# Two of six weight units per expert loaded ahead into spare memory and copied into the ring, with the refills of the spare memory issued behind the ring's loads from the fourth expert on

## The chip, the core and the metric

The kernel runs on one core of a Trainium2 chip. The metric is the device time of one launch in microseconds (us), the median of several runs. TensorE (PE) does the matrix products, VectorE (DVE), ScalarE (ACT) and GpSimd (POOL) the elementwise work. Each engine runs its own list of instructions in order and waits on semaphores for the others. SyncE (SP) issues most of the transfers from device memory (HBM) into the on-chip memory.

## What is computed

Two layers of a backbone over 128 context and 512 latent tokens of width 1024, all in float32. Each layer is an attention and convolution part, and then a mixture of 16 experts that choose their own tokens. The change is in the mixture:

```python
def expert_choice(h, w_router, w_gate, w_up, w_down):
    B, T, D = h.shape
    C = EC_FACTOR * T // N_EXPERTS
    aff = jax.nn.softmax(jnp.einsum('btd,de->bte', h, w_router).astype(jnp.float32), axis=-1)
    gsel, idx = lax.top_k(aff.transpose(0, 2, 1), C)
    xs = jax.vmap(lambda hb, ib: hb[ib])(h, idx)
    hid = jax.nn.silu(jnp.einsum('becd,edf->becf', xs, w_gate)) * jnp.einsum('becd,edf->becf', xs, w_up)
    ye = jnp.einsum('becf,efd->becd', hid, w_down) * gsel[..., None].astype(h.dtype)
    return jax.vmap(lambda yb, ib: jnp.zeros((T, D), yb.dtype).at[ib.reshape(-1)].add(yb.reshape(-1, D)))(ye, idx)
```

Each expert picks C = 64 latent and 16 context tokens, 80 columns together. It has three matrices of 1024 x 1024 float32, six times 2 MB. All 16 experts of both layers are read once, 192 units of 2 MB.

## The kernel before, in words

**Units and the ring.** An expert's weights come in six units of 2 MB: 0 is the first half of w_gate, 1 the first half of w_up, 2 and 3 the second halves, 4 and 5 the halves of w_down. I write e.i for unit i of expert e. The ring (`weight_ring`) has six slots of 2 MB, and unit i always goes to the slot `UNIT_SLOTS[l][i]` of layer l. So e.i can be loaded when TensorE is done with (e-1).i, which it tells through the semaphore `expert_used`.

**SP** first issues the six units of expert 0, while the attention part still runs. It stores and reloads the chosen token numbers (`picks`, `pick_row`) and the gains. Then a hardware loop over experts 1 to 15 waits for `expert_used` and issues one unit after the other (`expert_unit`, L404), always in the order 0 to 5.

**TensorE** runs, for each expert, `gate_up(e)` (units 0 to 3, 128 matmuls each, L868), waits for `picked_lo_ready` and `picked_hi_ready` ahead of it, and then `down(e)` (units 4 and 5, L885), whose first half waits for the hidden values (`hid_ready`).

**ScalarE**, for each expert, in order: wait until unit 2 is used, two SiLU operations over the gate's products (L1145, L1147); wait until unit 3 is used, then gather 48 of the next expert's 80 token columns (`pick_hi(e + 1)`, L1139).

**VectorE** multiplies SiLU by the up products (`gated_hidden`, L1554), scales the result (`gated_result`, L1569), and adds 48 of the 80 result columns onto the tokens (`add_hi`, L1578). **GpSimd** gathers the other 32 columns (`pick_lo`, L1699) and adds 32 of the result columns (`add_lo`, L1710). For every 8 columns an engine first loads 8 token numbers into registers (L322).

**After the last expert** of layer 0 the tokens are transposed back and layer 1 begins. After that of layer 1, the final norm (L558, L1158, L1596, L1605) is computed with the gain row in `x_norm`, which was loaded at the start of the expert stage, and the result is stored.

Of the kernel before, what the change touches and what calls it, by code (L numbers as in the profile page):

```python
# [17 lines left out]
EXPERTS, D_EXP = 16, 1024  # L18
# [42 lines left out]
PICK_SPLIT = 32  # L61
PICK_LOAD = 8

# [14 lines left out]
def build(nc, x_prompt, x_sample, c, cache_k, cache_v, c_ctx, norm1_g, w_mod, b_mod, w_in, conv_w, conv_b,  # L78
# [9 lines left out]
    with ctx:  # L88
# [32 lines left out]
        result_t = u_gate[:, 2 * D:2 * D + KD * CAP].rearrange("p (k n) -> p k n", k=KD)  # L121
# [7 lines left out]
        x_tile_flat = x_tile[:, :, :].rearrange("p b n -> p (b n)")  # L129
        pick_row = x_tile_flat[0:1, 0:EXPERTS * CAP].bitcast(u32)  # L130
        result_gain = x_tile_flat[:, EXPERTS * CAP:EXPERTS * CAP + KD * CAP].rearrange("p (k n) -> p k n", k=KD)
# [12 lines left out]
        cos_sb = sb("cos_sb", [P, N_LAT])  # L144
        sin_sb = sb("sin_sb", [P, N_LAT])
# [12 lines left out]
        o_tok_flat = o_tok[:, :, :, :].rearrange("p b h n -> p (b h n)")  # L158
        lam_rows = o_tok_flat[:, 0:DEPTH * 4 * HD].rearrange("p (l f n) -> p l f n", l=DEPTH, f=4)
# [50 lines left out]
        expert_used = signal("expert_used", 6 * EXPERTS)  # L210
        mod_rows_done = signal("mod_rows_done", len(MOD_LIST[0]))
# [71 lines left out]
        picks_loaded = signal("picks_loaded", 1, 16)  # L283
# [35 lines left out]
        def picks_of(engine, e, at, n):  # L319

            src = top_i[0:1, at:at + n] if e == 0 else pick_row[:, e * CAP + at:e * CAP + at + n]
            return nc.values_load_multi_w_load_instructions(  # L322
                src, engines=[engine], min_val=0, max_val=(N_LAT if at < CAP_LAT else N_CTX) - 1,
                skip_runtime_bounds_check_because="max_index counts within the row that it searched")[1]

# [54 lines left out]
        def _(sp):  # L380
# [21 lines left out]

            def expert_unit(l, e, i):
# [5 lines left out]
            for l in range(DEPTH):  # L409
# [50 lines left out]

                sp.wait_ge(*top_round.at(l, TOP_ROUNDS))
# [3 lines left out]
                sp.dma_start(pick_row, picks.rearrange("(a e) n -> a (e n)", a=1)).then_inc(picks_loaded.sem, 16)  # L465
# [18 lines left out]
        def _(pe):  # L484
# [20 lines left out]
            def past_transposes():  # L505

                pe.wait_ge(*misc_loaded.at(0, 4 * DEPTH + 3 * DEPTH + 2))
# [395 lines left out]
        def _(act):  # L903
# [27 lines left out]
            for l in range(DEPTH):  # L931
# [199 lines left out]
                def pick_hi(e):  # L1131

                    for at in range(PICK_SPLIT, CAP, PICK_LOAD):
                        if e == 0:
                            act.wait_ge(*top_round.at(l, at // 8 + 1))
                        elif e == 1 and at == PICK_SPLIT:
                            act.wait_ge(*picks_loaded.at(l, 1))
# [27 lines left out]
        def _(dve):  # L1165
# [27 lines left out]
            def setup_lambda():  # L1193

                dve.wait_ge(*misc_loaded.at(0, 4 * DEPTH + 3 * DEPTH + 2))
# [20 lines left out]
            for l in range(DEPTH):  # L1216
# [120 lines left out]
                def rotate(i):  # L1337
                    x = (k_t, q_t)[i][:, :, N_CTX:N_TOK]
                    for h in range(H):
# [3 lines left out]
                    nc.vector.tensor_tensor(x, x, cos_sb[:].unsqueeze(1).to_broadcast([P, H, N_LAT]), ALU.mult)  # L1343
                    own(step(nc.vector.tensor_tensor(rope_tmp, rope_tmp,
                                                     sin_sb[:].unsqueeze(1).to_broadcast([P, H, N_LAT]), ALU.mult)))
# [235 lines left out]
                dve.wait_ge(*picks_loaded.at(l, 1))  # L1581
# [29 lines left out]
        def _(pool):  # L1611
# [25 lines left out]
            def load_misc():  # L1637
# [10 lines left out]
                pool.dma_start(cos_sb[:], rope_cos).then_inc(misc_loaded.sem, 16)  # L1648
# [120 lines left out]
```

## Time and profile before

| | us |
|---|---|
| median of 3 runs | 1874.3 |
| the three runs | 1874.30, 1870.84, 1879.41 |
| the profiled execution | 1873.58 |
| its span in the trace | 1871.8 |
| expert stage of layer 0, first matmul to last | 442.8 to 931.4 |
| expert stage of layer 1, first matmul to last | 1356.3 to 1844.9 |

The two expert stages take 977 of the 1872 us. In the profile's 40 slices of 46.8 us each they are slices 10 to 19 and 30 to 39. There the moved bytes per second stand at one level, and TensorE's busy share is 8 or 9 tenths. The views to read are the slices, the chain of work that ended last, the timeline of SP and of TensorE, and the wait times; the rows are two sections below.

### The profile page before, as it was taken

Reading aid. Unit: us, or ns where it says so; the run is one execution under the profiler, and the core shown is the slowest. Engines: PE = TensorE matmul, PEld = TensorE weight load, DVE = VectorE, ACT = ScalarE, POOL = GpSimd, SP = SyncE. Lnnn points to the kernel's source line nnn. Section 1 sums busy time; section 2 is a strip of 40 time slices with the busy share of each in tenths; the row PEclk is TensorE's granted clock in tenths of the full one; section 3 lists DMA queues with packets and bytes.
Section 4 is the critical chain, followed back from the end, with each engine's and each line's share of the span. In section 5 each row is a group of like instructions: output and inputs, shape, how many; then the busy total and the mean of one; then the engine's idle time right before and its main releaser. Section 6 shows DMA issues by size and latency. Waiting matters only on the chain. (4 is left out here: it accounts for less than half of the span.)

```text
span 1871.8 us, 69942 instructions
## 1 busy us (share of the span) xinstructions
PE 1651.7 (88%) x27933; PEld 1303.6 (70%) x27933; DVE 815.4 (44%) x2591; ACT 446.5 (24%) x2106; POOL 373.3 (20%) x2131
## 2 busy tenths in 40 slices
PE   6999988996999888888859999889599998888885
PEld 3555456455999888888745444665389988888885
DVE  2299477244323323222245983853623232323233
ACT  2200155322221212121130012552312212121211
POOL 1100000001333423232210000000123333333331
PEclk9999989997999999999979999999799999999998
DMA  9447540224999999999921551320389999999992
GB/s 349 126 167 240 209 169 1 101 83 179 400 409 409 409 409 409 409 409 407 369 106 45 180 184 62 149 87 26 118 324 410 409 409 409 409 409 409 409 407 105
DMA packets 145011, 502.04 MB, mean 268 GB/s; under 512 B 4643, under 2 KB 5060, under 8 KB 144870
## 3 DMA queue, kind: packets, MB, share of 16 engines
q1 hardware_dynamic: 140740, 488.95, 67.3%
q0 software_dynamic: 3104, 10.36, 1.7%
q10 hardware_dynamic: 1026, 1.25, 0.2%
q8 instruction: 39, 0.64, 0.1%
q14 instruction: 102, 0.84, 0.1%
HBM read 494.23 MB, written 6.31 MB: 267 GB/s over the span
## 5 line engine op out<-in xcount | busy, mean ns | idle before, releaser
L868 PE MATMUL ps<-v_sb,weight_ring 128*64 128x80 f32 x16384 | 592.4, 234 | 70.7 <-DMA weight_ring<-in_w_gate_dram 26.6
L868 PEld LDWEIGHTS ps<-v_sb,weight_ring 128*64 128x64 f32 x16384 | 576.6, 138 | 86.2 <-DMA weight_ring<-in_w_gate_dram 33.2
L885 PE MATMUL ps<-v_sb,weight_ring 128*64 128x80 f32 x8192 | 296.4, 233 | 33.9 <-DVE v_sb L1554 19.6
L885 PEld LDWEIGHTS ps<-v_sb,weight_ring 128*64 128x64 f32 x8192 | 287.2, 137 | 43.1 <-DVE v_sb L1554 25.4
L640 PE MATMUL ps<-mix,weight_ring 128*128 128x128 f32 (+1 forms) x976 | 270.0, 437 | 4.4 <-DVE mix L1258 3.2
L1578 DVE TENSOR_TENSOR qk<-qk,u_gate 128x8 f32 x1536 | 209.2, 188 | 97.6 <-issue 95.9
L1139 ACT ACTIVATE v_sb<-mix 128x8 f32 x1536 | 187.1, 205 | 231.9 <-PE ps L868 150.9
L1699 POOL COPY v_sb<-mix 128x8 f32 x1024 | 143.0, 198 | 490.1 <-PE ps L868 432.9
L640 PEld LDWEIGHTS ps<-mix,weight_ring 128*128 128x128 f32 x976 | 147.5, 193 | 126.3 <-issue 121.0
L1710 POOL TENSOR_TENSOR qk<-qk,u_gate 128x8 f32 x1024 | 184.3, 219 | 212.3 <-DVE u_gate L1569 199.2
L1330 DVE SCALAR_TENSOR_TENSOR weight_ring<-u_gate,conv_cols,weight_ring 128x655 f32<-128x655 f32 x240 | 195.3, 894 | 0.0
L1554 DVE TENSOR_TENSOR v_sb<-v_sb,ps 128x320 f32<-128x320 f32 x64 | 28.3, 484 | 314.8 <-PE ps L868 314.8
L1569 DVE TENSOR_TENSOR u_gate<-ps,x_tile 128x320 f32<-128x320 f32 x64 | 31.5, 492 | 286.2 <-PE ps L885 286.2
L779 PE MATMUL ps<-weight_ring,mix 128*128 128x512 f32 x320 | 143.1, 603 | 0.0
L1145 ACT ACTIVATE v_sb<-ps 128x320 f32<-128x320 f32 x32 | 14.0, 438 | 522.0 <-PE ps L868 522.0
L779 PEld LDWEIGHTS ps<-weight_ring,mix 128*128 128x128 f32 x320 | 60.7, 194 | 71.1 <-issue 71.1
L677 PE MATMUL ps<-weight_ring,mix 128*128 128x512 f32 x160 | 70.5, 595 | 0.0
L1401 DVE TENSOR_REDUCE neg_m<-ps 128x2 f32<-128x1280 f32 (+1 forms) x40 | 50.8, 1274 | 16.1 <-PE ps L714 15.5
L1060 ACT ACTIVATE weight_ring<-ps,neg_m 128x640 f32<-128x640 f32 (+1 forms) x80 | 55.8, 707 | 3.2 <-DVE neg_m L1401 3.2
L677 PEld LDWEIGHTS ps<-weight_ring,mix 128*128 128x128 f32 x160 | 29.7, 190 | 36.5 <-issue 36.5
L1635 POOL DMA_DIRECT2D x_tile<-x_res x5 | 2.9, 574 | 250.9 <-PE ps L537 170.7
L725 PE MATMUL ps<-ident,weight_ring 128*128 128x128 f32 x168 | 33.4, 305 | 18.7 <-DVE o_tok L1420 9.0
(179 smaller groups left out, 1150.3 us busy)
## 6 DMA issues: line engine op xcount, KB each, us to landing
weight_ring<-in_w_gate_dram SPq DMA_DIRECT2D x64, 2048.0 KB, 23.8
weight_ring<-in_w_up_dram SPq DMA_DIRECT2D x64, 2048.0 KB, 23.8
weight_ring<-in_w_down_dram SPq DMA_DIRECT2D x64, 2048.0 KB, 24.5
weight_ring<-in_w_mod_dram SPq DMA_DIRECT2D x24, 2048.0 KB, 8.5
weight_ring<-in_w_in_dram SPq DMA_DIRECT2D x10, 2048.0 KB, 10.8
weight_ring<-in_w_out_dram SPq DMA_DIRECT2D x4, 2048.0 KB, 9.4
x_tile<-x_res POOLq DMA_DIRECT2D x5, 512.0 KB, 3.6
out_dram<-mix SPq DMA_DIRECT2D x5, 512.0 KB, 3.2
```

What stands on the lines that cost most here:

```text
L640: last = nc.tensor.matmul(ps[:, 2 * (n % 3) + bank, 0:cols.stop - cols.start], w[:, k, tokens(b)], mix[:, k, cols], start=(k == 0), stop=( ...
L677: last = nc.tensor.matmul(ps[:, 2 * (n % 3), :], mix[:, k, tokens(t)], w[:, k, :], start=(k == 0), stop=(k == KD - 1))
L779: last = nc.tensor.matmul(ps[:, 2 * (i % 2) + n, :], mix[:, k, tokens(t)], w[:, k % 4, n * BANK:(n + 1) * BANK], start=(at == 0), stop=(at ...
L868: last = nc.tensor.matmul(ps[c * HALF:(c + 1) * HALF, 2 * (i % 2) + f // BLK, f % BLK * CAP:(f % BLK + 1) * CAP], w[:, kk, o:o + HALF], pi ...
L885: last = nc.tensor.matmul(ps[c * HALF:(c + 1) * HALF, 4 + d // BLK, d % BLK * CAP:(d % BLK + 1) * CAP], w[:, kk, o:o + HALF], hid[:, k, :] ...
L1060: last = nc.scalar.activation(prob[:, b, m, 0:n], score_rows(s)[:, m, :], ACT.Exp, bias=neg_m[:, b, m:m + 1], accum_out=row_sum[:, b, m:m ...
L1139: last = nc.scalar.activation(picked_t[:, :, j:j + 1], picked_row(j, pick), ACT.Copy)
L1330: ins = nc.vector.scalar_tensor_tensor(acc[:, j, :], src, w, acc[:, j, :], ALU.mult, ALU.add)
L1401: nc.vector.tensor_reduce(neg_m[:, s % 2, :], score_rows(s), AX, ALU.max, negate=True)\
L1578: last = nc.vector.tensor_tensor(x, x, result_t[:, :, j:j + 1], ALU.add)
L1699: last = nc.gpsimd.tensor_copy(picked_t[:, :, j:j + 1], picked_row(j, pick))
L1710: last = nc.gpsimd.tensor_tensor(x, x, result_t[:, :, j:j + 1], ALU.add)
```

## The change

Three things are joined.

**Relayed units.** Units 0 and 1 of experts 1 to 15 are no longer loaded straight into the ring. SP loads each as four pieces of 512 KB (one DMA each) into eight buffers of 128 x 1024 (`relay`), made of a new tensor `spare`, the rotary tables' memory, `o_tok`, and parts of `u_gate`, `x_tile`, `conv_tmp` and `x_norm` that are idle in this stage. When TensorE has used unit r of expert e-1, ScalarE copies the four pieces into the ring slot (`relay_copy(e, r)`) and then raises `expert_loaded[r]`. The relays of expert 1 are issued before the experts begin. The relays of expert e+1 (`refill_relays(e + 1)`) are issued ahead of units 2 to 5 of expert e for e below 4, and behind them from e = 4 on (`RELAY_FIRST`). Since the rotary tables are overwritten, GpSimd reloads them in layer 1, and the gain row of the final norm is loaded after the last expert.

**Evened last adds.** For the last expert the 80 result columns are split 40 and 40 instead of 32 (GpSimd) and 48 (VectorE) (`LAST_SPLIT`).

**Early index registers.** `add_hi` and `add_lo` load the first 8 token numbers ahead of the wait for the result. The token numbers lie in four partitions, loaded by four small DMAs instead of one, and the result tile moves from `u_gate` to `v_sb`.

```diff
+LAST_SPLIT = 40
+RELAYS = 2
+RELAY_FIRST = 4
+RELAY = KD // 2
...
+        relay = ((spare[:, 0, :], spare[:, 1, :], rope_sb[:, :, :].rearrange("p b n -> p (b n)"), o_tok_flat),
+                 (u_gate[:, EXPERTS * CAP:EXPERTS * CAP + D], x_tile[:, 1, :], conv_tmp_flat[:, 0:D], x_norm[:]))
...
+            def relay_piece(l, e, r, j):
+                sp.dma_start(relay[r][j], expert_src(l, e, r)[:, j, :]).then_inc(relay_loaded[r].sem, 16)
...
+                for r in range(RELAYS):
+                    if r == 1:
+                        sp.wait_ge(*x2_ready.at(l, TILES))
+                        sp.wait_ge(*ssq2_ready.at(l, TILES))
+                        sp.wait_ge(*x2_transposed.at(l, TILES - 1))
+                    for j in range(RELAY):
+                        relay_piece(l, 1, r, j)
...
-                with sp.Fori(1, EXPERTS) as e:
-                    for i in range(6):
-
+                def refill_relays(e):
+
+                    for r in range(RELAYS if e < EXPERTS else 0):
+                        for j in range(RELAY):
+                            if j < RELAY - 1:
+                                sp.wait_ge(*relay_copied[r].at(l, (e - 2) * (RELAY - 1) + j + 1))
+                            else:
+                                sp.wait_ge(*expert_loaded[r].at(l, e))
+                            relay_piece(l, e, r, j)
+
+                for e in range(1, EXPERTS):
+                    if e < RELAY_FIRST:
+                        refill_relays(e + 1)
+                    for i in range(RELAYS, 6):
                         sp.wait_ge(*expert_used.at(l, e * 6 + (i - 5)))
                         expert_unit(l, e, i)
+                    if e >= RELAY_FIRST:
+                        refill_relays(e + 1)
...
+                def relay_copy(e, r):
+                    act.wait_ge(*expert_used.at(l, (e - 1) * 6 + r + 1))
+                    act.wait_ge(*relay_loaded[r].at(l, e * RELAY))
+                    w = ring[:, UNIT_SLOTS[l][r], :].rearrange("p (j n) -> p j n", j=RELAY)
+                    for j in range(RELAY - 1):
+                        nc.scalar.activation(w[:, j, :], relay[r][j], ACT.Copy).then_inc(relay_copied[r].sem, 1)
+                    nc.scalar.activation(w[:, RELAY - 1, :], relay[r][RELAY - 1], ACT.Copy)\
+                      .then_inc(expert_loaded[r].sem, 16)
+
                 pick_hi(0)
                 for e in range(EXPERTS):
+                    if e + 1 < EXPERTS:
+                        for r in range(RELAYS):
+                            relay_copy(e + 1, r)
                     act.wait_ge(*expert_used.at(l, e * 6 + 3))
...
                 def add_hi(e):
-                    dve.wait_ge(*result_taken.at(l, e + 2))
-                    for at in range(PICK_SPLIT, CAP, PICK_LOAD):
-                        for j, pick in enumerate(picks_of(mybir.EngineType.DVE, e, at, PICK_LOAD), at):
+                    for at in range(add_split(e), CAP, PICK_LOAD):
+                        rows = picks_of(mybir.EngineType.DVE, e, at, PICK_LOAD)
+                        if at == add_split(e):
+                            dve.wait_ge(*result_taken.at(l, e + 2))
+                        for j, pick in enumerate(rows, at):
...
+            pool.wait_ge(*expert_loaded[1].at(DEPTH - 1, EXPERTS))
+            pool.dma_start(x_norm[:], final_norm_g.rearrange("(a n) -> a n", a=1).to_broadcast([P, D]))\
+                .then_inc(gain_loaded.sem, 16)
```

**Where the instructions stand, ScalarE.** First ScalarE between the last gather for one expert and the first gather for the next, before the change. `v_sb<-mix` is one gathered column, `v_sb<-ps` a SiLU, `x_tile` the load of token numbers into registers.

```order
L1139 ACTIVATE v_sb<-mix 128x8
L1145 ACTIVATE v_sb<-ps 128x320 [waits expert_used]
L1147 ACTIVATE v_sb<-ps 128x320
L322 TENSOR_LOAD x_tile [waits expert_used]
L1139 ISA
```

And after the change, at the same place:

```order
L1178 ACTIVATE v_sb<-mix 128x8
L1186 ACTIVATE weight_ring<-spare 128x1024 [waits relay_loaded0,expert_used]
L1186 ACTIVATE weight_ring<-spare 128x1024
L1186 ACTIVATE weight_ring<-rope_sb 128x1024
L1187 ACTIVATE weight_ring<-o_tok 128x1024
L1186 ACTIVATE weight_ring<-u_gate 128x1024 [waits relay_loaded1,expert_used]
L1186 ACTIVATE weight_ring<-x_tile 128x1024
L1186 ACTIVATE weight_ring<-conv_tmp 128x1024
L1187 ACTIVATE weight_ring<-x_norm 128x1024
L1196 ACTIVATE v_sb<-ps 128x320 [waits expert_used]
L1198 ACTIVATE v_sb<-ps 128x320
L332 TENSOR_LOAD x_tile [waits expert_used]
```

Eight copies of 128 x 1024 and two waits for landed relays now stand ahead of the two SiLU operations; the copies are of the next expert's units, the SiLU is the present expert's.

**SP.** The second place is SP's expert loop. Before, one pass of the hardware loop:

```order
L404 ISA [waits expert_used]
L404 DMA weight_ring<-in_w_gate_dram 128x4x1024
L473 REGISTER_ALU
L404 DMA weight_ring<-in_w_up_dram 128x4x1024 [waits expert_used]
L473 REGISTER_ALU
L404 ISA [waits expert_used]
L404 DMA weight_ring<-in_w_gate_dram 128x4x1024
L473 REGISTER_ALU
L404 DMA weight_ring<-in_w_up_dram 128x4x1024 [waits expert_used]
L473 REGISTER_ALU
L404 DMA weight_ring<-in_w_down_dram 128x4x1024 [waits expert_used] x2
```

After the change, one pass for an expert e from 4 on (units 2 to 5 of e, then the pieces of units 0 and 1 of e+1):

```order
L420 DMA weight_ring<-in_w_gate_dram 128x4x1024 [waits expert_used]
L420 DMA weight_ring<-in_w_up_dram 128x4x1024 [waits expert_used]
L420 DMA weight_ring<-in_w_down_dram 128x4x1024 [waits expert_used] x2
L417 DMA spare<-in_w_gate_dram 128x1024 [waits relay_copied0] x2
L417 DMA rope_sb<-in_w_gate_dram 128x1024 [waits relay_copied0]
L417 DMA o_tok<-in_w_gate_dram 128x1024 [waits expert_loaded0]
L417 DMA u_gate<-in_w_up_dram 128x1024 [waits relay_copied1]
L417 DMA x_tile<-in_w_up_dram 128x1024 [waits relay_copied1]
L417 DMA conv_tmp<-in_w_up_dram 128x1024 [waits relay_copied1]
L417 DMA x_norm<-in_w_up_dram 128x1024 [waits expert_loaded1]
```

Units 0 and 1 of the next expert have moved from the head of the next pass to the end of this one, as eight transfers, and they wait for ScalarE's copies instead of for TensorE.

## Rows read from the trace of the kernel before

**Rows 1.** The page: busy time by engine, then the 40 slices.
```profile
PE 1651.7 (88%) x27933; PEld 1303.6 (70%) x27933; DVE 815.4 (44%) x2591; ACT 446.5 (24%) x2106; POOL 373.3 (20%) x2131
PE   6999988996999888888859999889599998888885
DMA  9447540224999999999921551320389999999992
```

**Rows 2.** Windows of layer 1's expert stage: us, busy by engine, PEclk, DMA share, GB/s.
```profile
1400.00:1500.00 100.00, 97.66 (x2792) 96.71 (x2788) 29.99 (x171) 26.52 (x200) 35.18 (x224) 1.00 1.03 409
1500.00:1840.00 340.00, 302.42 (x8340) 292.12 (x8334) 100.42 (x582) 66.97 (x502) 108.04 (x672) 1.00 1.00 397
```

**Rows 3.** Chain of work that ended last, layer 1: start us, us, what.
```profile
1418.04 17.87 PE ps L868 x512
1435.94 0.50 DVE v_sb L1554
1436.48 9.07 PE ps L885 x256
...
1815.14 24.97 DMA weight_ring<-in_w_down_dram
1840.23 4.67 PE ps L885 x128
1844.92 0.50 DVE u_gate L1569
```

**Rows 4.** Timeline of SP, the first issue of layer 1's loop.
```profile
1363.44 0.41 SPq L404 DMA_DIRECT2D weight_ring<-in_w_gate_dram  x1
```

**Rows 5.** Line L404 at 1318.7, alone in the queue; then at 1363.4.
```profile
L404 SPq DMA_DIRECT2D weight_ring<-in_w_down_dram x1: 367/367/367, 1318.7 to 1318.7; - x1
...
DMA to landing us min/median/max: 7.6/7.6/7.6
...
L404 SPq DMA_DIRECT2D weight_ring<-in_w_gate_dram x1: 405/405/405, 1363.4 to 1363.4; - x1
...
DMA to landing us min/median/max: 8.9/8.9/8.9
```

**Rows 6.** ScalarE's groups by form: busy us, mean ns of one, idle before.
```profile
L1145 ACT ACTIVATE v_sb<-ps 128x320 f32<-128x320 f32 x32 | 14.0, 438 | 522.0 <-PE ps L868 522.0
L1094 ACT ACTIVATE x_norm<-x_tile 128x1024 f32<-128x1024 f32 x10 | 10.5, 1046 | 27.8 <-DVE x_tile L1462 27.8
```

**Rows 7.** Windows around idle TensorE: after layer 0's last expert, at layer 1's first.
```profile
931.40:934.40 3.00, 0.00 (x0) 0.00 (x0) 1.69 (x10) 0.00 (x0) 1.67 (x10) 1.00 1.05 396
934.40:937.50 3.10, 0.00 (x0) 0.00 (x0) 2.29 (x16) 0.00 (x0) 2.81 (x17) 0.51 1.03 376
...
1356.30:1361.00 4.70, 4.70 (x70) 4.70 (x72) 0.83 (x1) 1.07 (x1) 0.00 (x0) 0.50 0.40 143
1361.00:1363.40 2.40, 2.40 (x72) 2.40 (x70) 0.00 (x0) 0.00 (x0) 0.00 (x0) 0.98 0.00 0
```

**Rows 8.** Timeline after the last expert of layer 1, GpSimd, VectorE, TensorE.
```profile
1846.18 1.54 POOL L1710 TENSOR_TENSOR qk<-qk,u_gate 128x8 f32 x8 [25.28 <-DVE u_gate L1569]
1846.19 1.08 DVE L1578 TENSOR_TENSOR qk<-qk,u_gate 128x8 f32 x8 [0.78 <-DVE u_gate L1569]
1848.01 4.48 POOL L1710 TENSOR_TENSOR qk<-qk,u_gate 128x8 f32 x24 [0.28 <-issue]
1853.20 1.00 DVE L1578 TENSOR_TENSOR qk<-qk,u_gate 128x8 f32 x8 [0.58 <-issue]
1854.78 1.00 DVE L1578 TENSOR_TENSOR qk<-qk,u_gate 128x8 f32 x8 [0.58 <-issue]
1855.92 4.53 PE L558 MATMUL ps<-ident,qk 128*128 128x128 f32 x24 [11.05 <-DVE qk L1578]
1859.12 0.15 DVE L1596 TENSOR_SCALAR mean_sq<-ssq 128x1 f32<-128x1 f32 x1 [3.34 <-ACT conv_tmp L1158]
```

**Rows 9.** DMA issues by line: KB each, us from issue to landing.
```profile
x_norm<-in_final_norm_g_dram POOLq DMA_DIRECT2D x1, 512.0 KB, 3.6
```

More of the change, by code:

```diff
@@ L143, in build @@
         o_sq = conv_tmp[:, 1, 0:BANK].rearrange("p (h n) -> p h n", h=H)
-        cos_sb = sb("cos_sb", [P, N_LAT])
-        sin_sb = sb("sin_sb", [P, N_LAT])
+        rope_sb = sb("rope_sb", [P, 2, N_LAT])
+        cos_sb, sin_sb = rope_sb[:, 0, :], rope_sb[:, 1, :]
+        spare = sb("spare", [P, 2, D])
         past_k_t = sb("past_k_t", [P, DEPTH, H, PAST])
@@ L210, in build @@
         expert_used = signal("expert_used", 6 * EXPERTS)
+        relay_loaded = [signal(f"relay_loaded{r}", RELAY * (EXPERTS - 1), 16) for r in range(RELAYS)]
+        relay_copied = [signal(f"relay_copied{r}", (RELAY - 1) * (EXPERTS - 1)) for r in range(RELAYS)]
+        rope_loaded = signal("rope_loaded", unit=16)
         mod_rows_done = signal("mod_rows_done", len(MOD_LIST[0]))
@@ L282, in build @@
         picks_stored = signal("picks_stored", 1, 16)
[L283 removed]
+        picks_loaded = signal("picks_loaded", 4, 16)
         gains_stored = signal("gains_stored", 1, 16)
@@ L319, in picks_of @@
         def picks_of(engine, e, at, n):
-            src = top_i[0:1, at:at + n] if e == 0 else pick_row[:, e * CAP + at:e * CAP + at + n]
+            row, col = STRIP * (e // 4), (e % 4) * CAP + at
+            src = top_i[0:1, at:at + n] if e == 0 else pick_rows[row:row + 1, col:col + n]
             return nc.values_load_multi_w_load_instructions(
@@ L324, in picks_of, with add_split @@
                 skip_runtime_bounds_check_because="max_index counts within the row that it searched")[1]
+        def add_split(e):
+            return PICK_SPLIT if e + 1 < EXPERTS else LAST_SPLIT
         def picked_row(j, pick):
@@ L464, in _ @@
                 sp.wait_ge(*picks_stored.at(l, 1))
-                sp.dma_start(pick_row, picks.rearrange("(a e) n -> a (e n)", a=1)).then_inc(picks_loaded.sem, 16)
+                for q in range(4):
+                    sp.dma_start(pick_rows[STRIP * q:STRIP * q + 1, :],
+                                 picks[4 * q:4 * q + 4, :].rearrange("(a e) n -> a (e n)", a=1))\
+                      .then_inc(picks_loaded.sem, 16)
                 sp.wait_ge(*gains_stored.at(l, 1))
@@ L1337, in rotate @@
                 def rotate(i):
+                    dve.wait_ge(*rope_loaded.at(0, 2 * (l + 1)))
                     x = (k_t, q_t)[i][:, :, N_CTX:N_TOK]
@@ L1579, in add_hi @@
                     last.then_inc(added_hi.sem, 1)
-                dve.wait_ge(*picks_loaded.at(l, 1))
+                dve.wait_ge(*picks_loaded.at(l, 4))
                 dve.wait_ge(*gains_loaded.at(l, 1))
@@ L1664, in _ @@
                     load_misc()
+                else:
+                    pool.wait_ge(*expert_loaded[0].at(l - 1, EXPERTS))
+                pool.dma_start(cos_sb, rope_cos).then_inc(rope_loaded.sem, 16)
+                pool.dma_start(sin_sb, rope_sin).then_inc(rope_loaded.sem, 16)
                 pool.wait_ge(*mod_cols_done.at(l, mod_groups(l)))
@@ L1702, in add_lo @@
                 def add_lo(e):
-                    pool.wait_ge(*result_taken.at(l, e + 2))
-                    if e > 0:
-                        pool.wait_ge(*added_lo.at(l, e))
-                        pool.wait_ge(*added_hi.at(l, e))
-                    for at in range(0, PICK_SPLIT, PICK_LOAD):
-                        for j, pick in enumerate(picks_of(mybir.EngineType.Pool, e, at, PICK_LOAD), at):
+                    for at in range(0, add_split(e), PICK_LOAD):
+                        rows = picks_of(mybir.EngineType.Pool, e, at, PICK_LOAD)
+                        if at == 0:
+                            pool.wait_ge(*result_taken.at(l, e + 2))
+                            if e > 0:
+                                pool.wait_ge(*added_lo.at(l, e))
+                                pool.wait_ge(*added_hi.at(l, e))
+                        for j, pick in enumerate(rows, at):
                             x = residual_row(j, pick)
```

24 lines of the change are left out of this document (9 added, 15 removed).

## The prediction

> **What bounds the kernel now.** I read the slices first. In both expert stages DMA stands at 9 tenths in every slice, and PE at 8 or 9 [rows 1]. The windows tell the two phases apart: up to 1500 TensorE is busy 97.66 of 100 us, later 302.42 of 340, while the transfers never pause [rows 2]. So TensorE lives at first on the six units that were loaded ahead, uses them up, and from 1500 on waits for each unit to land. The chain confirms it: one expert takes TensorE 17.87 + 0.50 + 9.07, with seams 27.5 us [rows 3], and the last link of the chain is a unit's landing, 4.67 us of matmuls, and VectorE [rows 3].
>
> The transfer side: the first unit of the loop is issued at 1363.44 [rows 4] and lands 8.9 us later, at 1372.3 [rows 5]. The last is issued at 1815.14 and lands at 1840.11 [rows 3]. Those are units 1 and 90 of layer 1's loop, so a unit takes 467.8 / 89 = 5.26 us, and six take 31.5 us, against TensorE's 27.5. **The stage ends when its 90 units are through, and only two things can shorten it: fewer units after the start, or an earlier start.**
>
> **The part that ought to gain.** Two units of expert 1 now land before the stage, in time when DMA is mostly idle (slices 28 and 29, digits 0 and 3 [rows 1]). 88 units are left: 2 x 5.26 = 10.5 us per layer. The stream can start only when ScalarE has copied the first relayed piece, one 128 x 1024 operation of 1.05 us [rows 6]; 9.5 us per layer would be left if the stream then stayed full.
>
> **Does it stay full? Experts 1 to 3: yes.** SP issues 2.0, 2.1, 1.2 to 1.5, 3.0, 3.1, 2.2 to 2.5, 4.0, 4.1, 3.2 to 3.5, then 4.2 to 4.5, 5.0, 5.1. With the first landing at 1373.3 and 5.26 us each, 3.2 lands at 1373.3 + 14 x 5.26 = 1446.9. Expert 2 begins at 1418.04 [rows 3] and expert 3 27.5 us later, at 1445.5, and wants 3.2 another 9 us later. So TensorE runs at its own 27.5 us and ScalarE finds the relays landed. Its work per expert grows by 8 copies, about 8 us, in a queue that is 24% busy [rows 1]; two copy groups of 3.9 us fit into the 4.5 us that each unit of matmuls takes. I price that at nothing. What hides it is TensorE's own unit time.
>
> **From expert 4 on: no.** ScalarE's list is in order, and the copies of the next expert's units 0 and 1 stand ahead of the present expert's SiLU. Both copies wait for landed relays, and from expert 4 on SP issues those relays behind all of the present expert's units. So down(e) cannot start before (e+1).1 has landed, three units after e.4, which TensorE wants next. Let X(e) be the landing of (e+1).1.
>
> - X(4) is the 24th landing: 1373.3 + 23 x 5.26 = 1494.2. Before, TensorE was at down(4) at 1418.04 + 2 x 27.5 + 17.9 = 1490.9.
> - After X: four copies. A 128 x 1024 operation takes 1.05 us [rows 6], and overlapped ones some 0.95 (an estimate: the operation less the part that the next one hides): 3.9 us. SiLU 0.44 [rows 6], VectorE's product 0.50 [rows 3], two hand-overs of 0.05. TensorE starts unit e.4 at X + 4.95.
> - e.4 takes 4.65 us. Its slot is then free, and SP, which has stood there, issues (e+1).4 after 0.15. By then the stream, which needed this issue when (e+1).3 began to drain, has only (e+1).3's tail left: X + 9.75 against the end of (e+1).3 at X + 10.5 (and with the clock term below, nothing).
> - Landing a unit from an empty queue took 7.6 and 8.9 us [rows 5]; I take the middle, 8.3, since the queue is nearly, not wholly, empty. Then (e+1).5, (e+2).0 and (e+2).1 follow at 5.26.
>
> **The loop closes:** X(e+1) = X(e) + 4.95 + 4.65 + 0.15 + 8.3 + 15.8 = X(e) + 33.85 us. That is 2.3 more than the stream's own 31.5, for every expert from 4 to 14.
>
> **TensorE's clock.** Per expert TensorE works 27 us and then stands for 6 to 7 us ahead of down(e). After layer 0's last expert it stood from 931.4, and the granted clock was 1.00 up to 934.4 and 0.51 after, that is 1.2 instead of 2.4 GHz [rows 7]. When layer 1's experts began it was at 0.50 for the first 4.70 us and 0.98 after [rows 7], and the first unit took until 1363.3 [rows 4], 7.0 instead of 4.65 us. I take it that the clock falls in each of these pauses and that e.4 pays 2.1 us, a little less than the 2.4 seen. The period is then 35.95 us. The Trainium skill's page "TensorE: Matmul & The Clock Gate", section "HAM oscillation — how this bites in real kernels", describes such a loop, in which every tile's wait for data puts the array back to half rate; the expert stage before the change shows granted clock 1.00 throughout [rows 2], so only the new pause can bring it.
>
> **The end of a stage.** X(14) = 1494.2 + 10 x 35.95 = 1853.7. Then 4.95 to down(14), 9.3 + 2.1 for it, and all of expert 15, whose weights now come early enough, at 27.5: 1897.6. Before it was 1844.9 [rows 3]. **+52.7 us in layer 1**, and the same in layer 0, whose stage had the same length (488.6 us both).
>
> A second page of the Trainium skill, "DMA: Bandwidth & Descriptors", bears on this in its section "Rules for kernel authors": issue early, compute, and wait on the semaphore late. ScalarE here waits early, ahead of work that others need. The section "Anatomy of one DMA" of that page of the Trainium skill puts the fixed cost of a transfer at about 2.0 us; by that the landing would be 5.26 + 2.0 = 7.3, the period 34.95, and each stage 10 us shorter than forecast, an estimate. The rows here show 7.6 and 8.9, and I stay with them.
>
> **Last adds and index registers.** VectorE added 48 columns from 1846.19 to 1855.8, 1.58 us for each 8 ([rows 8], 1853.20 to 1854.78), and GpSimd was through with its 32 at 1852.5. With 40 and 40, VectorE saves one group, 1.6 us, and the register load ahead of the first, 0.6 of the 0.78 idle [rows 8]; GpSimd needs 6.3 / 4 = 1.6 more and starts 0.6 earlier, so it ends at about 1853.5. The end moves by 2.2 us in each layer. In layer 1 the gain row is now issued by GpSimd when it is done, and took 3.6 us to land [rows 9]; VectorE wants it 3.3 us after the last add ([rows 8], 1855.8 to 1859.12). So 0.5 us is given back there. Sum: -2.2 - 1.7 = -3.9. Elsewhere the early registers lie beside waiting.
>
> **Edits at no cost.** Four picks DMAs instead of one: SP is 1 us later with the gains, which VectorE needs only for down(0), 20 us later. Reloading the rotary tables: 512 KB at the start of layer 1, where DMA shows digits 2, 1 and 5 [rows 1], long ahead of their use.
>
> **Sum:** profiled execution 1873.6 + 2 x 52.7 - 3.9 = 1975.1. Its time is within 1 us of the median 1874.3, so I forecast the same for a median.
>
> **Rivals.**
> 1. *The clock holds at 2.4 GHz* through the pauses. Then the period is 33.85 and the stage ends at 1494.2 + 338.5 + 4.95 + 9.3 + 27.5 = 1874.5, +29.6 per layer: 1873.6 + 59.2 - 3.9 = 1929. For it: the pause is 6 to 7 us, and the pause in the rows was 11. Against: it had fallen 3 us into that one [rows 7].
> 2. *The loop hides in the stream*: a free slot is reported just early enough and each issue overlaps what is in flight. The period is 31.5; TensorE is still three units behind the stream at the end: 1494.2 + 315.4 + 4.95 + 9.3 + 27.5 = 1851.4, +6.5 per layer, 1883. The issue would have to come 3 us before the stream needs it; it comes 0.8 us before.
> 3. *Faster*: ScalarE is not in the way, because the stream at expert 4 is already three units further ahead than I reckon, and stays there. Then 2 x 9.5 + 3.9 us are gained: 1851. It decides at X(4): 5.1 would have to land before 1490.9 - 4.95 = 1486, 8 us earlier than reckoned. In the rows TensorE gains 4 us per expert on the stream, so such a lead melts within three experts. That speaks against it.
> 4. *The relays do not run ahead at all*, for want of a free buffer. The order of waits gives no reason.
>
> **How the numbers follow.** Forecast 0.66, rival 1 0.22, rival 2 0.05, rival 3 0.06, rest 0.01. For the range: low side with no clock loss, 7.6 for the landing and 5.13 per unit (2.1 MB at the 409 GB/s of [rows 2]): period 32.7, +18 per layer, 1906. High side with 8.9 for the landing, 2.4 for the clock and copies that don't overlap (4.2): period 37.15, +65 per layer, 1873.6 + 130 - 3.9 = 2000. So 1908 to 2000. Faster by over 0.5% (what a measurement of this kernel can tell) 0.07, within 0.5% 0.03, slower 0.90.
>
> **What would show it.** In the timeline of an expert from 5 on: ScalarE idle until a relay has landed, copies, and only then SiLU; TensorE idle 6 to 7 us ahead of each down, none between units; a period of 36 us; the granted clock below 1 in these pauses; DMA share under 1 in slices that were full; SP's waits for `expert_used` long, and its issues short. Experts 1 to 3 at 27.5 us. I would be wrong if TensorE waited for units and not for hidden values, or if DMA stayed at its level to the end.

## The result and the profile after

| | before, us | after, us |
|---|---|---|
| median of 4 runs | 1873.16 | 1985.28 |
| lowest to highest | 1870.84 to 1879.41 | 1979.50 to 1991.72 |
| the profiled execution, and its span | 1873.58, 1871.8 | 1987.45, 1985.5 |

The ratio is 1.0599, with a 95% interval from 1.0572 to 1.0625: **slower by 6%**. Forecast were 1975 us, with 1908 to 2000 as the range. The spans differ by 113.7 us.

The page of the changed kernel, as in [rows 1]: busy time by engine, then the slices, here of 49.6 us, with PEclk, the granted clock in tenths.

```profile
PE 1682.6 (85%) x27933; PEld 1349.1 (68%) x27933; DVE 819.4 (41%) x2575; ACT 668.8 (34%) x2346; POOL 390.8 (20%) x2149
PE   6999988958988788788859999899599778778786
PEclk9999988979988989889979999999799879988888
DMA  9346342059999989989831552121699989989982
```

TensorE does the same 27933 matmuls, but takes 31 us longer for them (1682.6 against 1651.7). PE has 7s where it had 8s and 9s. ScalarE has 240 instructions more, the copies: 15 experts x 8 x 2 layers. DMA shows 8s among the 9s.

Layer 1's expert stage in windows, as in [rows 2]. Columns: us, busy PE, PEld, DVE, ACT, POOL, granted clock, DMA share, GB/s. The first is experts 3 and 4 up to the first pause, the second runs from there to just behind the last relay's landing (1916.28).

```profile
1504.00:1551.00 47.00, 44.06 (x1264) 43.66 (x1260) 16.55 (x102) 17.78 (x62) 18.00 (x105) 1.00 1.01 395
1551.00:1917.00 366.00, 291.96 (x7680) 289.30 (x7680) 93.41 (x530) 139.87 (x582) 107.12 (x643) 0.88 0.89 346
```

Before, the stream ran at a share of 1.00 and 397 GB/s to the end. Now it does so only until TensorE stops for the first time; from there on 346 GB/s and a clock of 0.88.

The chain of work that ended last, as in [rows 3]: start us, us, what.

```profile
1448.33 17.76 PE ps L907 x512
1466.65 9.07 PE ps L924 x256
1475.73 17.87 PE ps L907 x512
...
1536.47 16.24 DMA x_norm<-in_w_up_dram
1557.65 11.11 PE ps L924 x256
1573.30 15.62 DMA x_norm<-in_w_up_dram
1593.87 11.74 PE ps L924 x256
1610.54 15.59 DMA x_norm<-in_w_up_dram
```

The rows from 1448.33 on are experts 1 and 2: experts 1 to 3 follow each other at 27.5 us (1448.33 to 1475.73 is 27.4), with matmuls alone. From expert 4 on the chain alternates: the last piece of the relayed unit 1 (`x_norm`), ScalarE, `down` (L924), again such a piece. These landings, the X(4) to X(14) of the prediction, are at 1552.71, 1588.93, 1626.13 and so on to 1916.28: ten periods in 363.57 us, 36.36 us each.

One period on TensorE and ScalarE, in their timelines: start us, us, what, and in brackets the idle time ahead and its releaser.

```profile
1557.65 11.08 PE L924 MATMUL ps<-v_sb,weight_ring 128*64 128x80 f32 x256 [9.01 <-DVE v_sb L1606]
1568.65 17.93 PE L907 MATMUL ps<-v_sb,weight_ring 128*64 128x80 f32 x512
1593.87 11.71 PE L924 MATMUL ps<-v_sb,weight_ring 128*64 128x80 f32 x256 [7.29 <-DVE v_sb L1606]
```
```profile
1583.90 2.00 ACT L1186 ACTIVATE weight_ring<-spare 128x1024 f32<-128x1024 f32 x2 [19.97 <-DMA o_tok<-in_w_gate_dram]
...
1589.01 1.06 ACT L1186 ACTIVATE weight_ring<-u_gate 128x1024 f32<-128x1024 f32 x1 [1.21 <-DMA x_norm<-in_w_up_dram]
...
1591.87 1.04 ACT L1187 ACTIVATE weight_ring<-x_norm 128x1024 f32<-128x1024 f32 x1
1592.81 0.41 ACT L1196 ACTIVATE v_sb<-ps 128x320 f32<-128x320 f32 x1
```

TensorE is done with the gate and up products at 1586.6 (1568.65 + 17.93). Their SiLU (L1196) runs at 1592.81, because ScalarE stands at the copy of the next expert's unit 1 until 1589.01 and then makes four copies. The wait is not one for weights: TensorE goes through the 512 matmuls of units 0 to 3 without a gap, and units 4 and 5 of this expert have landed too (1572.15 and 1578.71, from the rows below).

SP's issues in the same period, then the two units of w_down on their way to landing.

```profile
1564.35 4.79 SPq L420 DMA_DIRECT2D weight_ring<-in_w_down_dram  x2
1573.30 1.20 SPq L417 DMA_DIRECT2D x_norm<-in_w_up_dram  x1
```
```profile
DMA to landing us min/median/max: 7.8/7.8/7.8
```
```profile
DMA to landing us min/median/max: 9.9/9.9/9.9
```

The first was issued at 1564.35, when TensorE had used unit 4 of the expert before, the second at 1568.77. Ahead of them the stream ran dry (columns as above):

```profile
1560.00:1562.00 2.00, 2.00 (x38) 2.00 (x36) 0.00 (x0) 1.35 (x12) 0.00 (x0) 0.54 0.39 156
1562.00:1564.00 2.00, 2.00 (x65) 2.00 (x61) 0.00 (x0) 1.52 (x14) 0.00 (x0) 1.00 0.02 6
1564.00:1566.00 2.00, 2.00 (x64) 2.00 (x60) 0.00 (x0) 0.00 (x0) 0.00 (x0) 1.00 0.24 33
```

By the three shares some 4.7 us of a full stream are missing here (an estimate), about what a period is longer than the stream's 31.5. SP had transfers that were free to go: ScalarE's copies had emptied all eight relay buffers by 1556.7 (1555.65 + 1.04), but their refills stand behind these two units in SP's list.

The clock, in a window on the end of this pause (1553 to 1558), in one on the next pause and in one on the `down` behind that (columns as above):

```profile
1553.00:1558.00 5.00, 0.35 (x6) 0.35 (x8) 0.89 (x2) 5.00 (x14) 1.75 (x13) 0.50 1.03 410
1589.00:1592.50 3.50, 0.00 (x0) 0.00 (x0) 0.00 (x0) 3.49 (x4) 2.62 (x20) 0.52 1.02 406
1592.50:1599.40 6.90, 5.53 (x84) 5.53 (x86) 0.88 (x2) 5.79 (x45) 0.63 (x5) 0.50 0.82 327
```

In each of the eleven pauses of layer 1, 6.3 to 9.0 us long, the granted clock falls to 0.50, the lower of its levels (1.2 GHz), and it stays there for the first 2.7 to 6.0 us of the work behind: `down` takes 10.3 to 11.9 us, 11.4 in the mean, instead of 9.07.

The waits summed over both layers: who waited for what, us, times, longest.

```profile
PE ps L924 <- DVE v_sb L1606: 168.6, 32, 9.0
...
ACT weight_ring L1186 <- DMA o_tok<-in_w_gate_dram: 441.1, 22, 21.2
```

**Where the 113.7 us are.** Layer 0's expert stage takes 549.4 us instead of 488.6 (+60.8), layer 1's 545.8 (+57.2). Between the stages it is 1.9 less, behind the last 2.1 less, ahead of the first 0.3 less: 118.0 - 4.3 = 113.7.

### The profile page after: what moved, and what is told of

Its sections match the earlier page's. It is cut to its first block and busy times, and to the rows that moved or that the text cites. A ratio compares the mean times of both kernels' runs of the same rounds, so it can differ in the third digit from the quotient of the medians.

```text
span 1985.5 us, 69965 instructions
## 1 busy us (share of the span) xinstructions
PE 1682.6 (85%) x27933; PEld 1349.1 (68%) x27933; DVE 819.4 (41%) x2575; ACT 668.8 (34%) x2346; POOL 390.8 (20%) x2149
## 5 line engine op out<-in xcount | busy, mean ns | idle before, releaser
L907 PE MATMUL ps<-v_sb,weight_ring 128*64 128x80 f32 x16384 | 579.0, 234 | 17.9 <-ACT v_sb L1178 15.6
L907 PEld LDWEIGHTS ps<-v_sb,weight_ring 128*64 128x64 f32 x16384 | 573.7, 138 | 21.9 <-issue 19.3
L924 PE MATMUL ps<-v_sb,weight_ring 128*64 128x80 f32 x8192 | 341.9, 254 | 173.5 <-DVE v_sb L1606 168.6
L924 PEld LDWEIGHTS ps<-v_sb,weight_ring 128*64 128x64 f32 x8192 | 336.0, 155 | 179.4 <-DVE v_sb L1606 173.8
L1768 POOL TENSOR_TENSOR qk<-qk,v_sb 128x8 f32 x1040 | 200.2, 234 | 361.4 <-DVE v_sb L1621 358.8
L1632 DVE TENSOR_TENSOR qk<-qk,v_sb 128x8 f32 x1520 | 212.1, 194 | 90.5 <-issue 89.7
L1186 ACT ACTIVATE weight_ring<-spare 128x1024 f32<-128x1024 f32 x60 | 60.1, 1049 | 493.7 <-DMA o_tok<-in_w_gate_dram 441.1
L1178 ACT ACTIVATE v_sb<-mix 128x8 f32 x1536 | 180.4, 205 | 87.1 <-issue 43.9
L1621 DVE TENSOR_TENSOR v_sb<-ps,x_tile 128x320 f32<-128x320 f32 x64 | 31.5, 492 | 321.7 <-PE ps L924 321.7
L1035 ACT ACTIVATE qk<-ps 128x512 f32<-128x512 f32 x16 | 9.6, 598 | 153.1 <-PE ps L679 153.1
## 6 DMA issues: line engine op xcount, KB each, us to landing
weight_ring<-in_w_gate_dram SPq DMA_DIRECT2D x34, 2048.0 KB, 11.9
```

Source lines behind the costliest of these rows:

```text
L907: last = nc.tensor.matmul(ps[c * HALF:(c + 1) * HALF, 2 * (i % 2) + f // BLK, f % BLK * CAP:(f % BLK + 1) * CAP], w[:, kk, o:o + HALF], pi ...
L924: last = nc.tensor.matmul(ps[c * HALF:(c + 1) * HALF, 4 + d // BLK, d % BLK * CAP:(d % BLK + 1) * CAP], w[:, kk, o:o + HALF], hid[:, k, :] ...
L1178: last = nc.scalar.activation(picked_t[:, :, j:j + 1], picked_row(j, pick), ACT.Copy)
L1186: nc.scalar.activation(w[:, j, :], relay[r][j], ACT.Copy).then_inc(relay_copied[r].sem, 1)
L1632: last = nc.vector.tensor_tensor(x, x, result_t[:, :, j:j + 1], ALU.add)
L1768: last = nc.gpsimd.tensor_tensor(x, x, result_t[:, :, j:j + 1], ALU.add)
```

## The experiments

Two readings were held against each other. **The loop:** ScalarE waits for the next expert's relays ahead of the present SiLU, SP issues those relays behind units that TensorE frees only after this SiLU, and so landing, copy, SiLU, `down` and issue make one closed chain that is longer than the stream needs. **The rivals:** the relays as such (eight small transfers, copies through ScalarE, traffic in the memories) cost the time; or the clock alone does. Ratios are against the kernel before, run on the same chip beside each.

### e1: the relays always first

```diff
-RELAY_FIRST = 4
+RELAY_FIRST = 16
```

> The changed kernel with one number changed: the relays of the next expert are issued ahead of the present expert's units 2 to 5 for all experts (RELAY_FIRST 16), as the changed kernel does for experts 1 to 3. All copies, pieces and waits stay. My theory (ScalarE's copies wait for relays that SP issues too late, and hold back SiLU): the relays have landed when ScalarE comes to them, no pause ahead of down, the stream of weights stays full, a period of 31.5 us. Unit 5 of expert 14 is the 84th to land in layer 1, at 1373.3 + 83 x 5.26 = 1809.9 on the clock of before, then 4.65 and 27.5 us of expert 15: 1842, 3 us less than before per layer, and 4 us less from the last adds: about 1862 us. Rival (the relaying itself is what costs: 8 us more of ScalarE's work per expert, 512 KB pieces, eight issues more on SP): it stays at 1950 us or more.

Measured: 1864.08 us (10 runs, 1857.61 to 1869.64), ratio 0.9954 (0.9934 to 0.9975). A single number of the change carries the whole loss: with the same relays, copies and buffers, and only SP's order undone, 1985 becomes 1864. The timeline of TensorE in one expert shows what bounds the stage then: TensorE waits a little for units to land, and hardly for the hidden values:

```profile
1634.85 4.65 PE L907 MATMUL ps<-v_sb,weight_ring 128*64 128x80 f32 x128 [1.72 <-DMA weight_ring<-in_w_gate_dram]
1640.85 4.65 PE L907 MATMUL ps<-v_sb,weight_ring 128*64 128x80 f32 x128 [1.34 <-DMA weight_ring<-in_w_up_dram]
1646.15 4.65 PE L924 MATMUL ps<-v_sb,weight_ring 128*64 128x80 f32 x128 [0.66 <-DVE v_sb L1606]
```

The large pause is gone, and the small ones, none over 2.6 us here, leave the granted clock high (window, columns as above):

```profile
1500.00:1840.00 340.00, 304.27 (x8426) 297.34 (x8422) 102.59 (x583) 144.97 (x582) 113.09 (x672) 0.99 0.97 384
```

So the relays as such do not cost the time.

### e4: the switch at expert 10

```diff
-RELAY_FIRST = 4
+RELAY_FIRST = 10
```

> The changed kernel with the relays moved behind from the tenth expert on instead of the fourth. My theory, with the period measured in the changed kernel (36.4 us): relay unit 1 of expert 11 is the 60th to land, at 1683.6 in layer 1 on the clock of before, four more periods to 1829.2, and 44.4 to the end: 1873.6, 29 us more than before per layer, about 1926 us. Experts up to 9 show no pause ahead of down. Rival (a fixed cost of having both orders, or of the switch): about what the changed kernel shows, 1985 us.

Measured: 1924.19 us (1 run), 52 us over the kernel before beside it: somewhat under half of the loss, with 5 of the 11 pauses. In layer 1 the periods up to X(9) are 30.7 to 31.7 us. X(10) comes 53.1 us after X(9), since the relays move behind four more units there, and from X(10) on the periods are 35.9 to 36.9. The first two pauses ahead of `down` in layer 1:

```profile
1712.27 10.88 PE L924 MATMUL ps<-v_sb,weight_ring 128*64 128x80 f32 x256 [13.99 <-DVE v_sb L1606]
...
1748.42 11.55 PE L924 MATMUL ps<-v_sb,weight_ring 128*64 128x80 f32 x256 [7.35 <-DVE v_sb L1606]
```

The loss begins at the expert at which the order changes, at 10 as at 4, and each later expert adds the same.

### e2: the copies behind the SiLU

SP's order stays as changed (`RELAY_FIRST` 4); ScalarE copies behind the SiLU and the gathers from expert 4 on.

```diff
-                    if e + 1 < EXPERTS:
+                    if e + 1 < EXPERTS and e < RELAY_FIRST:
                         for r in range(RELAYS):
                             relay_copy(e + 1, r)
...
+                    if e + 1 < EXPERTS and e >= RELAY_FIRST:
+                        for r in range(RELAYS):
+                            relay_copy(e + 1, r)
```

> The changed kernel, with SP's order kept, but ScalarE's copies for experts 5 to 15 placed behind SiLU and the gathers of the pass instead of ahead of them. My theory: nothing waits for a landed relay any more that TensorE doesn't need itself, so the stream stays full: the 88th unit lands at 1373.3 + 87 x 5.26 = 1830.9 in layer 1 on the clock of before, TensorE lags it by 2 to 3 us since the last copies take 4 us, and ends at 1838, 7 us less than before per layer; with 4 us from the last adds about 1856 us. Rival (relays behind the ring's loads cost because of their place in SP's queue, whoever copies them when): it stays above 1950 us.

Measured: 1871.64 us (10 runs, 1863.61 to 1878.87), ratio 1.0008 (0.9989 to 1.0027). The loop is cut from its other side: the period is 31.5 us in layer 1 (X(4) 1493.94, X(14) 1808.64), and 114 us come back. So it takes both, SP's order and ScalarE's early wait. But the time is 15.6 us above what I had expected. TensorE and ScalarE around the last two experts show why:

```profile
1786.29 17.93 PE L907 MATMUL ps<-v_sb,weight_ring 128*64 128x80 f32 x512 [3.22 <-ACT weight_ring L1187]
...
1817.12 17.93 PE L907 MATMUL ps<-v_sb,weight_ring 128*64 128x80 f32 x512 [3.23 <-ACT weight_ring L1187]
```
```profile
1812.33 0.95 ACT L1178 ACTIVATE v_sb<-mix 128x8 f32 x8 [0.40 <-issue]
1813.18 1.99 ACT L1186 ACTIVATE weight_ring<-spare 128x1024 f32<-128x1024 f32 x2
```

The relays of unit 0 lie there (the last landed at 1803.52), but ScalarE first gathers 48 columns, from 1804.9 to 1813.2, and then copies for 3.9 us. TensorE stands 3.2 us ahead of each expert for the copy of unit 0 and so falls behind the stream: the stage ends 15 us after the last landing (1829.87 to 1844.70). I had left the gathers out of the sum.

### e6 and e7: the copies behind fewer gathers

e6 is e2 with the gathers for the next expert split 40 and 40 between ScalarE and GpSimd. e7 is e6 with both moves only from expert 12 on.

```diff
+GATHER_SPLIT = 40
...
-                    for at in range(PICK_SPLIT, CAP, PICK_LOAD):
+                    for at in range(GATHER_SPLIT, CAP, PICK_LOAD):
...
-RELAY_FIRST = 4
+RELAY_FIRST = 12
```

> As e2_copies_late (ScalarE copies behind its gathers from the pass of expert 4 on), and the 80 gathered columns split 40 to GpSimd and 40 to ScalarE instead of 32 and 48. In e2 TensorE stood 3.2 us ahead of every expert, since ScalarE copied unit 0 only when its 48 gathers were done. 8 gathers fewer take 1.6 us off: the pause falls to 1.6 us or less, an expert to 29.1 us, under the stream's 31.6, so TensorE follows the stream and ends some 7 us after the last landing instead of 15. About 6 us less than before per layer and 4 from the last adds: 1857 us. Rival (the gathers are not what the copies wait for): as e2, 1872 us.

> As e6_late_even, with both moves (relays behind the ring's loads, copies behind the gathers) made from expert 12 on instead of from 4 on. Up to expert 11 the relays run ahead as in e1_ahead, which keeps the stream full with no pause; the last four experts then get their units in the order in which TensorE uses them, which takes away what e1_ahead still lost at the end (all of expert 15 after the last landing of expert 14). By the same sum as e6: 1856 us. Rival (the switch costs a pause in which the stream runs dry once): 1862 us, as e1_ahead.

Measured: e6 1853.03 us (4 runs), ratio 0.9897 (0.9863 to 0.993); e7 1851.15 us (4 runs, 1847.59 to 1854.64), ratio 0.9884 (0.9847 to 0.9921). TensorE ahead of an expert, in e6 and then in e7:

```profile
1614.74 4.65 PE L908 MATMUL ps<-v_sb,weight_ring 128*64 128x80 f32 x128 [1.79 <-ACT weight_ring L1188]
```
```profile
1800.22 4.65 PE L908 MATMUL ps<-v_sb,weight_ring 128*64 128x80 f32 x128 [2.04 <-ACT weight_ring L1188]
```

Eight gathers fewer on ScalarE take the pause from 3.2 us to between 1.5 and 1.8 us (four experts of layer 1, from 1527 to 1615), until TensorE has caught up with the stream. From 1646 on e6's pauses are 1.8 to 3.4 us, but ScalarE's copy now starts as soon as the relay has landed (1642.10 and 1642.19). The stage ends 6.7 us after the last landing (1825.68 to 1832.42) instead of 15, and the time is 18.6 us below e2, which shows that e2's missing gain lay in ScalarE's queue. e7 beats both kernels, by 1.2% and, by the medians, 6.8%. Whether it is better than e6 the four runs of each don't tell.

### e8: one relayed unit

```diff
-RELAYS = 2
+RELAYS = 1
```

> The changed kernel with one relayed unit instead of two (RELAYS 1): only unit 0 of the next expert goes through the spare memory, unit 1 is loaded straight into the ring. The order on ScalarE and on SP stays. My theory: the loop from the end of unit 4 over SP's issue, the landings of e.4 and e.5 and of one relayed unit, the copies and SiLU is one unit shorter (36.4 - 5.3 = 31.1 us), just under the stream's own 31.5, so the period falls to 31.5 to 31.8; TensorE is still two units behind the stream at the end. The one relay of expert 15 is the 84th landing, 1810.7 in layer 1 on the clock of before, and 44 us follow: 1855, 10 us more than before per layer, about 1889 us. Rival (the cost goes with the number of relayed units): half of the loss, about 1929 us. Pauses ahead of down stay in both.

Measured: 1883.48 us (1 run). This takes one unit out of the loop and leaves the order as changed. X is here the landing of unit 0. A window of layer 1 (columns as above) and TensorE in it:

```profile
1550.00:1800.00 250.00, 224.15 (x6082) 222.12 (x6079) 73.15 (x414) 79.97 (x432) 82.64 (x499) 0.95 1.01 400
```
```profile
1659.98 11.42 PE L924 MATMUL ps<-v_sb,weight_ring 128*64 128x80 f32 x256 [4.67 <-DVE v_sb L1606]
```

TensorE still waits for the hidden values ahead of all eleven `down`s, and nine of the eleven are slow. But the loop is one landing shorter, so it is no longer than the stream's own period, and costs nothing by itself: X comes every 31.58 us (ten periods from 1497.44 to 1813.26), at a full DMA share. What is left over the kernel before, 11 us, fits the late end: a stage takes 495.5 us instead of 488.6, and 43.2 of them come after the last X, the last `down` of the loop and a whole expert. So this wait at a low clock did no harm while the transfers never ran dry.

### e9 and e3: the clock kept up

How much of a period is the clock? After each expert's gate and up products TensorE gets extra matmuls into an unused bank, which fill most of the pause; the output isn't touched. e9 adds 7 calls of 512 columns, in all experts:

```diff
+                def idle_work():
+                    for j in range(IDLE_WORK):
+                        nc.tensor.matmul(ps[:, 6, :], ones[:], past_v[:, l, :], start=True, stop=True)
+
                     gate_up(e)
+                    idle_work()
```

> The changed kernel with 7 more matmuls of 512 columns (14 instructions of 0.45 us, 6.3 us) into an unused bank behind gate_up of every expert, so that TensorE works through most of the pause ahead of down with few instructions. If the low clock is what makes down take 11.1 to 11.9 us, the granted clock stays at 1.00 in experts 5 to 14, down takes 9.07 us and the period falls from 36.4 to about 34.1 us. Rival (down is slow for another reason): the period stays at 36.4 with down at 11 to 12 us. The total is no test: the added work makes experts 0 to 4 and 15 longer by 6.3 us each, some 23 us of it on the path per layer, so it would be about 1985 us by the first and about 2030 by the second.

Measured: 1989.31 us (1 run). TensorE in one period:

```profile
1633.94 6.28 PE L935 MATMUL ps<-past_v,ones 128*128 128x512 f32 x14
1641.66 9.07 PE L925 MATMUL ps<-v_sb,weight_ring 128*64 128x80 f32 x256 [1.44 <-DVE v_sb L1612]
```

```profile
1600.00:1700.00 100.00, 95.80 (x2263) 84.52 (x2263) 27.76 (x159) 38.87 (x172) 32.01 (x192) 1.00 0.94 362
```

`down` is back at 9.07 us and the granted clock at 1.00 (the window, columns as above), and the period falls from 36.36 to 34.3 us (X(4) 1567.61, X(14) 1910.76). So the clock costs 2.0 us per period, 20 of the 57 us of a stage. The pause is still there (6.3 filled, 1.4 idle), and so is the loop: 34.3 is some 2.8 above the 31.5 of e1 and e2. The total did not fall because the 6.28 us are paid in full where there is no pause: X(4) comes 155.5 us after the stage's start instead of 137.8, and what follows X(14) takes 2.7 us more.

e3, earlier, was to do the same with 176 small calls (80 columns) in a second hardware loop over experts 4 to 15.

```diff
+IDLE_WORK = 176
...
+                with nc.Fori(0, RELAY_FIRST, engines=[mybir.EngineType.PE], hint_back_edge=True) as e:
...
+                with nc.Fori(RELAY_FIRST, EXPERTS, engines=[mybir.EngineType.PE], hint_back_edge=True) as e:
                     gate_up(e)
+                    idle_work()
```

> The changed kernel with 176 more matmuls of the expert's own size (80 columns, 64 rows of output) into an unused bank, behind gate_up of each expert from the fourth on, so that TensorE works through most of the pause ahead of down. They take 176 x 36 ns = 6.4 us of a pause of 7 to 9. TensorE's loop is split in two for it. If the low clock after the pause is what makes down take 11.1 to 11.9 us instead of 9.07, the granted clock stays at 1.00, down takes 9.07 again and the period falls from 36.4 by about 2.3 to 34.1 us: 23 us less per layer, but 6.4 more in expert 15, which has no pause, and up to 4 for the second loop's first pass: 1950 to 1960 us. Rival (down is slow for another reason, such as the copies' or the transfers' traffic): the period stays at 36.4 and the time rises to about 1998 us.

Measured: 2302.34 us (1 run). It says nothing on the clock. The 176 calls stand in the trace as 352 matmuls, so the filling was 12.7 us and not 6.4, and in the second loop TensorE waited for its own instructions. Its main group over the whole run (busy us, mean ns, idle ahead), a piece of its timeline, and the instruction queue's packets, MB and share:

```profile
L908 PE MATMUL ps<-v_sb,weight_ring 128*64 128x80 f32 x16384 | 630.5, 241 | 142.9 <-issue 126.6
```
```profile
1713.19 4.12 PE L908 MATMUL ps<-v_sb,weight_ring 128*64 128x80 f32 x57 [3.77 <-issue]
```
```profile
q8 instruction: 267, 4.37, 0.8%
```

The changed kernel has 0.62 MB in that queue. The test of the clock is e9, with 14 matmuls instead of 352.

### e5: last adds and index registers alone

The kernel before, with the adds of the last expert split 40 and 40 and the first 8 token numbers loaded ahead of the wait.

```diff
+LAST_SPLIT = 40
...
-                    dve.wait_ge(*result_taken.at(l, e + 2))
-                    for at in range(PICK_SPLIT, CAP, PICK_LOAD):
-                        for j, pick in enumerate(picks_of(mybir.EngineType.DVE, e, at, PICK_LOAD), at):
+                    for at in range(add_split(e), CAP, PICK_LOAD):
+                        rows = picks_of(mybir.EngineType.DVE, e, at, PICK_LOAD)
+                        if at == add_split(e):
+                            dve.wait_ge(*result_taken.at(l, e + 2))
+                        for j, pick in enumerate(rows, at):
```

> The kernel before with the small parts alone: 40 and 40 columns for the last expert, and the first 8 token numbers loaded ahead of the wait. No relays. VectorE ends 2.2 us earlier in each layer, and the gain row is loaded early as before: 4.4 us less, about 1869 us. Rival (GpSimd becomes the later one and takes it back): no difference.

Measured: 1868.29 us (12 runs, 1860.08 to 1875.00), ratio 0.9977 (0.9958 to 0.9996): 3.7 us less than the 1872.01 of the kernel before beside it. The interval allows 0.7 to 7.9 us, and the 4.4 that it was priced at lies in it; the part has nothing to do with the loss. Of e1's 7.9 us gain over the kernel before, some 4 would then be the relays' own, by difference.

## Why the prediction was right, step by step

The mechanism is the one forecast, and the size nearly so: the spans differ by 113.7 us where 101.5 were forecast, 4.5 too few in layer 1, 8.1 in layer 0, and 0.4 less outside the stages.

- **The way to the first pause.** X(4), the 24th landing, was put 137.9 us after the stage's start. It came after 137.8 (1414.92 to 1552.71) in layer 1 and 139.2 in layer 0. Experts 1 to 3 at 27.5 us: yes.
- **From the landing to SP's issue.** Put at 4.95 + 4.65 + 0.15 + 2.1 for the clock, 11.85 us; the ten periods of layer 1 show 11.88 in the mean (10.91 to 12.48). The copies, SiLU and product took 4.94 (1552.71 to 1557.65). With 4.94 and 4.65 + 0.15 taken off, 2.1 is left for the clock, as forecast from the one slow unit of [rows 7]; the whole `down` was 2.3 slower in the mean, and e9's period 2.0 shorter. The Trainium skill's page "TensorE: Matmul & The Clock Gate", section "HAM oscillation — how this bites in real kernels", was named for a penalty that is paid once in every pass; the trace agrees, with all eleven `down`s slow.
- **From the issue to the next landing: the term that was too small.** Put at 8.3 + 3 x 5.26 = 24.1 us, it was 24.5 in the mean (23.7 to 25.0). The first unit landed sooner, after 7.8 us, but the second came 6.4 us behind it in the mean (5.2 to 7.2), not 5.26, which is the spacing before, where the share stood at 1.00. The relays then took 10.3 for the two. So two errors stood against each other, and that the sum is off by only 0.4 is in part luck. In ten periods it makes 4 us of the 4.5 by which layer 1's stage was longer than forecast (57.2 against 52.7); the other 0.5 lies around the last `down`. The Trainium skill's page "DMA: Bandwidth & Descriptors", section "Anatomy of one DMA", gives 2.0 us as a fixed cost for transfers that GpSimd issues, while these are issued by SP. The period worked out by it in the prediction, 34.95 us, is not what the trace shows (36.36).
- **Layer 0** was 8.1 us longer than forecast, nearly all by its period (36.65, 7.0 us in ten) and by X(4) (1.3 us). There the way from the issue to the next landing took 24.7 us in the mean; why more than in layer 1 stays open.
- **The tails.** Put at -3.9, they and the stretch between the stages gave -4.3. VectorE's last group now ends at 1969.4 beside GpSimd's 1968.95. The gain row was to give back 0.5 us (from the 3.6 and 3.3 us of the prediction's own rows 0.3 would follow); it gave 0.1:

```profile
1961.39 7.56 POOL L1768 TENSOR_TENSOR qk<-qk,v_sb 128x8 f32 x40 [21.42 <-DVE v_sb L1621]
1968.42 1.00 DVE L1632 TENSOR_TENSOR qk<-qk,v_sb 128x8 f32 x8 [0.57 <-issue]
1968.88 0.60 POOL L1781 DMA_DIRECT2D x_norm<-in_final_norm_g_dram  x1
1972.76 0.15 DVE L1650 TENSOR_SCALAR mean_sq<-ssq 128x1 f32<-128x1 f32 x1 [3.34 <-DMA x_norm<-in_final_norm_g_dram]
```

  In this timeline of the end the row is issued at 1968.88, half a microsecond ahead of VectorE's last add, since GpSimd was done first; it landed at 1972.69, and ScalarE's sum of squares at 1972.65.
- **The range.** Its lower sum came to 1906, and the range began at 1908; nothing hangs on it.
- **The rivals.** That the clock holds (1929) fell by the windows at 0.50. That the loop hides in the stream (1883) is false for two relayed units and true for one: a stage is 6.9 us longer in e8, where this rival had 6.5. That ScalarE is not in the way (1851) is false as the kernel is written; e7 reaches about that time (1851.15), but by another way, with the wait moved.

## What to carry to other kernels

Where an engine works its list in order, a wait for a prefetch belongs behind all work that others need from it now (e2), or the prefetch must be issued well ahead of it (e1). Trace both ends of such a wait: if the transfer it waits for is issued only after something that this engine has yet to release, the chain is closed, and its length, not the bandwidth, sets the period. Compare that length with the stream's period: here a chain shorter by one transfer cost almost nothing in a pass (e8), and the one that was 3 us longer than the stream's period cost that in each pass, with the 2 us of the clock on top.

## What was not expected of the hardware

- **With the longer loop body TensorE waited for instructions.** With 352 matmuls and their weight loads more in a hardware loop over experts, beside 768 and theirs, e3 read 4.37 MB of instructions instead of 0.62, and TensorE stood 126.6 us for "issue" ahead of its main group. The split into two loops is not by itself the reason: in the first loop of e3, with the short body, the queue moved 0.10 MB from 450 to 570 us, in the second 1.59 MB from 600 to 1100. The changed kernel and e9, with 14 more, read 0.62 and 0.64 MB. Where between the two lengths it begins was not tried.
- **Behind a stream that had run dry, the second 2 MB unit comes late too**: issued 4.4 us after the first, it landed 6.4 us after it in the mean, where units before landed every 5.26. The relays are issued right behind it; how much of this is their share of the stream was not told apart.
- **Pauses of nearly the same length did and did not bring the clock down.** Those of 6.3 to 9.0 us took it to 0.50 each time, and the two of 4.7 us in e8 did as well (`down` 11.42 and 11.57 us). Of e8's pauses of 2.4 to 3.0 us most did (`down` 10.72 us behind one of 2.50) and two did not (9.07 behind 2.61 and 2.96). e1's, of 0.3 to 2.6 us several times per expert, left it at 0.99 in the mean.
